# A two-block model in one kernel: the second attention's third turned group placed behind the scores' first 512 columns, and the convolution's high parts made in the first two units

## The reference, cut to what matters

```python
def diff_attend(q, k, v, lam):
    s = jnp.einsum('bqhmd,bkhmd->bhmqk', q, k, preferred_element_type=jnp.float32)
    a = jax.nn.softmax(s * (1.0 / math.sqrt(ATTN_HEAD_DIM)), axis=-1)
    a = a[:, :, 0] - lam * a[:, :, 1]
    return jnp.einsum('bhqk,bkhe->bqhe', a.astype(v.dtype), v)

def head_out(o, subln_g, lam_init):
    return (rmsnorm_2(o, subln_g) * (1.0 - lam_init)).reshape(b, t, ATTN_V_W)
...
    attn = head_out(latent_diff_attention(q, k_all, v_all, lam), subln_g, lam_init)
    conv = short_conv(gb, gc, xc, conv_w)
    out = jnp.einsum('btn,nd->btd', jnp.concatenate([attn, conv], axis=-1), w_out)
```

## Time and profile before

| | us |
|---|---|
| median of three runs | 2697.93 (2696.41 to 2701.72) |
| the profiled execution | 2696.95 |
| its span | 2695.7 |
| TensorE busy in the span | 2598.3 (96%) |
| VectorE busy | 1829.8 (68%) |
| ScalarE busy | 1304.7 (48%) |
| GpSimd busy | 515.2 (19%) |

### The profile page before, as it was taken

How to read it: one execution, slowest core, us unless ns; L and a number is a source line. 1 busy time by engine, 2 the same in 40 slices (tenths; PEclk the granted TensorE clock), 3 DMA queues, 4 the chain that set the end, 5 groups by cost and what they waited for, 6 DMA issues and landing times. The chain is left out here.

```text
span 2695.7 us, 35795 instructions
## 1 busy us (share of the span) xinstructions
PE 2598.3 (96%) x13421; PEld 2202.4 (82%) x13421; DVE 1829.8 (68%) x2193; ACT 1304.7 (48%) x2014; POOL 515.2 (19%) x729
## 2 busy tenths in 40 slices
PE   8999999999999999999999999999997799999996
PEld 7799998888898787778888898778876688888885
DVE  4288887632458888875557333489845788888887
ACT  4255653511343333333445121288723477777775
POOL 5722220000022222221101310022233100000102
PEclk9999999999999999999999999999998899999998
DMA  8700001111323445657655422001144699999998
GB/s 299 268 25 25 24 21 40 47 47 50 123 100 107 148 151 176 198 178 287 202 194 173 110 61 67 5 21 36 67 150 192 236 386 395 395 396 394 395 394 271
DMA packets 249515, 461.90 MB, mean 171 GB/s; under 512 B 16588, under 2 KB 138176, under 8 KB 247936
## 3 DMA queue, kind: packets, MB, share of 16 engines
q1 hardware_dynamic: 218944, 352.73, 37.3%
q0 software_dynamic: 30288, 106.84, 12.1%
q10 hardware_dynamic: 112, 0.03, 0.0%
HBM read 384.79 MB, written 65.32 MB: 167 GB/s over the span
## 5 line engine op out<-in xcount | busy, mean ns | idle before, releaser
L508 PE MATMUL ps<-r,r 128*128 128x512 f32 (+4 forms) x10508 | 2302.0, 377 | 9.1 <-DVE r L672 3.8
L508 PEld LDWEIGHTS ps<-r,r 128*128 128x128 f32 (+1 forms) x10508 | 1879.7, 188 | 360.3 <-issue 9.6
L485 ACT ACTIVATE r<-f 128x2048 fp32r<-128x2048 f32 (+2 forms) x339 | 503.8, 1495 | 386.3 <-PE ps L508 383.2
L3739 DVE TENSOR_TENSOR r<-f,r 128x2048 fp32r<-128x2048 f32 x188 | 429.2, 2291 | 63.8 <-ACT r L485 62.4
L493 DVE TENSOR_TENSOR r<-f,r 128x1024 fp32r<-128x1024 f32 (+1 forms) x151 | 168.1, 1128 | 319.0 <-ACT r L485 319.0
L508 PE MATMUL ps<-f,f 128*128 128x128 f32 (+1 forms) x1218 | 153.3, 277 | 3.9 <-ACT f L1288 3.3
L508 PEld LDWEIGHTS ps<-f,f 128*128 128x128 f32 x1218 | 145.0, 193 | 6.8 <-issue 5.6
L876 DVE SCALAR_TENSOR_TENSOR f<-f,misc,f 128x1023 f32<-128x1023 f32 (+29 forms) x120 | 146.4, 1260 | 0.0
L2018 ACT ACTIVATE r<-f 128x512 fp32r<-128x512 f32 x140 | 87.1, 629 | 71.2 <-PE ps L508 57.4
L3757 POOL DMA_INDIRECT ff_scratch<-f,misc x15 | 29.0, 1934 | 474.1 <-ACT f L3868 442.4
L3269 DVE TENSOR_REDUCE misc<-ps 128x1 f32<-128x1280 f32 x64 | 95.1, 1487 | 21.6 <-PE ps L508 21.3
(11 more groups left out here) (349 smaller groups left out, 2282.8 us busy)
## 6 DMA issues: line engine op xcount, KB each, us to landing
f<-in_w_gate_dram SPq DMA_DIRECT2D x64, 1024.0 KB, 8.3
f<-in_w_up_dram SPq DMA_DIRECT2D x64, 1024.0 KB, 10.1
f<-in_w_down_dram SPq DMA_DIRECT2D x64, 1024.0 KB, 8.0
f<-in_w_in_dram SPq DMA_DIRECT2D x56, 512.0 KB, 4.4
f<-in_w_ada_dram SPq DMA_DIRECT2D x96, 256.0 KB, 4.8
f<-in_w_ffn_in_dram SPq DMA_DIRECT2D x80, 256.0 KB, 4.0
hid_scratch<-f POOLq DMA_DIRECT2D x77, 256.0 KB, 2.8
f<-hid_scratch SPq DMA_DIRECT2D x35, 512.0 KB, 5.0
```

The costliest lines, as they stand in the source:

```text
L485: self.act.activation(hi, raw, ACT.Copy).then_inc(self.sem(st.name + "_hi"), 1)
L508: return self.pe.matmul(o, left, right, start=start, stop=stop, skip_group_check=True)
L3739: self.dve.tensor_tensor(es.lo[i % 4], es.raw[i % 8], es.hi[i % 4].bitcast(F32), ALU.subtract).then_inc(self.sem("e_lo"), 1)
```

## The change

Two edits. On TensorE, in slots 2 to 31, the three transposed groups no longer stand together: groups 0 and 1 come first, then the first 512 columns of the scores of map 1 (two matmuls), then group 2, then the other score columns. On ScalarE the four high parts of the convolution, so far one at the end of each of slots 0 to 3, are made two at the end of slot 0 and two in slot 1 ahead of the second exponential. The semaphores and their counts stay. The orders of VectorE, GpSimd and SyncE are the same as before.

```diff
@@ -3101,31 +3101,32 @@
     def score_sums(self, mp):
         return self.ps[:, 3 * mp:3 * mp + 3, :].rearrange("p a b -> p (a b)")[:, 0:1280]
 
-    def pe_scores2(self, u, mp):
+    def pe_scores2(self, u, mp, parts=(0, 1, 2)):
         pe, sem = self.pe, self.sem
         h, i = self.PAIRS[u]
         sk = self.stacks[h % 2]
-        if u:
+        if u and parts[0] == 0:
             pe.wait_ge(*sem(f"a2_exp{mp}", u))
-        if i == 0:
+        if i == 0 and parts[0] == 0:
             pe.wait_ge(*sem("sk_hi", 6 * (h + 1)))
             pe.wait_ge(*sem("sk_lo", 6 * (h + 1)))
             pe.wait_ge(*sem(f"dma_k{h}", 96))
         q = sk["Q"][mp][:, i * P:(i + 1) * P]
-        for c in range(3):
+        for c in parts:
             cs = slice(c * 512, min(c * 512 + 512, 1280))
             o = self.ps[:, 3 * mp + c, 0:cs.stop - cs.start]
             self.mm(o, q, sk["K"][mp][:, cs], True, False)
             t = self.mm(o, q, sk["L"][mp][:, cs] if c < 2 else sk["C"][mp], False, True)
-        t.then_inc(sem(f"a2_qk{mp}"), 1)
+        if parts[-1] == 2:
+            t.then_inc(sem(f"a2_qk{mp}"), 1)
 
     def pe_attention2(self):
         pe, sem, ps = self.pe, self.sem, self.ps
         n = len(self.PAIRS)
 
-        def turn_p(u):
+        def turn_p(u, groups):
             pe.wait_ge(*sem("a2_mix", u + 1))
-            for g in range(3):
+            for g in groups:
                 k = self.turn_use("p", u, g)
                 self.pe_turn_bank(k)
                 w = (4, 4, 2)[g]
@@ -3160,9 +3161,14 @@
             if u == 2:
 
                 pe.wait_ge(*sem("c2_o", 8))
-            if 2 <= u <= n + 1:
-                turn_p(u - 2)
-            if 0 < u < n:
+            if 2 <= u < n:
+                turn_p(u - 2, (0, 1))
+                self.pe_scores2(u, 1, (0,))
+                turn_p(u - 2, (2,))
+                self.pe_scores2(u, 1, (1, 2))
+            elif n <= u <= n + 1:
+                turn_p(u - 2, (0, 1, 2))
+            if u == 1:
                 self.pe_scores2(u, 1)
             elif u >= n:
                 self.pe_wout2_part(u - n, 1)
@@ -3222,6 +3228,11 @@
                 act.wait_ge(*sem("a2_om", u - 1))
             act.activation(self.SQ2, self.OM2[j], ACT.Square, accum_out=self.sub_ss[j]).then_inc(sem("a2_sq"), 1)
 
+        def high_conv(first, last):
+            for m in range(first, last):
+                ct = (m + 3) % 4
+                act.activation(self.MX[0][:, 4 + ct, :], self.CV[ct], ACT.Copy).then_inc(sem("mc_hi"), 1)
+
         def high_o(u):
             h, i = self.PAIRS[u]
             k = self.turn_use("o", u)
@@ -3248,16 +3259,16 @@
                 elif parts and u > 2:
                     act.wait_ge(*sem("mc_lo", u - 1))
                 self.act_stack(h, parts)
+            if u == 1:
+                high_conv(2, 4)
             if u < n:
                 expo(u, 1)
             if 2 <= u <= n + 1:
                 copy_v(u - 2)
-            if u < 4:
-                if u == 0:
-                    act.wait_ge(*sem("c2_o", 8))
-                    act.wait_ge(*sem("cv2_mm", 24))
-                ct = (u + 3) % 4
-                act.activation(self.MX[0][:, 4 + ct, :], self.CV[ct], ACT.Copy).then_inc(sem("mc_hi"), 1)
+            if u == 0:
+                act.wait_ge(*sem("c2_o", 8))
+                act.wait_ge(*sem("cv2_mm", 24))
+                high_conv(0, 2)
             if u in (3 * NT + 3, 3 * NT + 5):
                 self.act_high_out((u - 3 * NT - 1) // 2)
 
```

## The result

| | median of runs, us | against the kernel before |
|---|---|---|
| before | 2699.96 (19 runs) | |
| changed | 2704.32 (19 runs) | 1.0016, 95% [1.0009, 1.0023] |

The account below looks back on a forecast made before the run. A two-unit loop of 12.69 us bounds the second attention, VectorE the stack slots; -2.15 - 0.25 + 1.47 - 0.4 + 1.1 + 1.2 = +1.0 gives 2697.9, 2698.9 with the runs' median; range 2690.5 to 2704.5.

Parts of the forecast that it names:

- rival 3: Second attention: the lock repeats in both free runs, +4.2, with slots 14 and 22 +7.2, 2702 to 2705; chance 0.2.
- What bounds the kernel: Second attention: a loop over two units of 12.69 us, 6.35 a unit; with stacks VectorE is busy 31.13 of 32.07.
- GpSimd late next: Without the copy wait, TensorE's turned output waits for GpSimd's last operation; loop 12.59, gaining 0.05 a unit, not 0.25.
- the lock repeats: VectorE's mix and GpSimd's last operation exclude each other on shared ports; pitches alternate 5.97 and 7.88, 6.93 a unit.
- 6.14: Pitch in us between first maxima of successive units below which the mix starts before GpSimd's last operation.
- The free runs: Slots 16 to 19: +1.1 (caught +2.5, not -0.3); slots 24 to 31: +1.2 (caught +3.0, not -0.7).
- TensorE's own pitch: Unit pitch after a stall with TensorE on its own: 5.97 us without the copy wait of 0.25, 6.22 with it.
- E + 3.7: TensorE's arrival at the turned output, counted from E, the second exponential's start on ScalarE; 1.04 behind the third group.
- The opening: Convolution's copies moved: -2.15, from 1.75 at M(3) (0.94 copy, 0.8 columns done early) and 0.4 of 0.87.
- Slots 9, 10, with stacks: Slot 9 at 5.97 for 6.22, -0.25; slot 10 caught, +1.47; VectorE-bound slots with stacks, -0.2 twice, -0.4.
- What would show it wrong: L3333 at 0.61 at pitches of 6.0, unit pitches without stacks of 6.0, or unit 1's exponential starting late.
- number 2: Second attention: GpSimd bounds the loop but the lock doesn't repeat, -4.8, 2693.1; chance 0.25.

Follow-up runs that it names:

- scale: Changed kernel with GpSimd's last operation of a unit (output scaled by its norm) made on ScalarE, behind the copies of the turned groups: 2696.86 us, ratio 0.9989.
- scale2: Changed kernel with that output scaling made on ScalarE between the second and third copy of a slot: 2692.05 us, ratio 0.9975 against the kernel before.
- maxfirst: Changed kernel with two VectorE operations swapped, the second maximum of a slot ahead of the mix: 2695.04 us, ratio 0.9987 against the kernel before.
- again2: Changed kernel with two superfluous score matmuls ahead of the first of map 1 in slots 2 to 31: 2705.40 us, ratio 1.002 against the kernel before.
- again1: Changed kernel with one superfluous score matmul ahead of the first of map 1 in slots 2 to 31: 2705.70 us, ratio 1.0024 against the kernel before.
- noeps: Changed kernel without GpSimd's first operation of a unit (the norm's epsilon), its factor put into ScalarE's square: 2700.63 us, ratio 1.0000 against the kernel before.
- part2: Kernel before with only the convolution's edit (high parts two in slot 0, two in slot 1): 2699.13 us, ratio 0.9999.
- part1: Kernel before with only the third group's edit (behind the scores' first 512 columns): 2706.14 us, ratio 1.0031.

## Why the prediction was right, and where it wasn't

The range held the time, by 0.2 us of its upper end (2704.5), which is luck in part, and the change lies within the 0.2% to which I gave 0.65. But what happened in the stage is the main part of rival 3, to which I gave 0.2: both free runs caught, +4.2 in its sum, +4.0 measured. The forecast change was +1.0 and the measured one is +4.4 (the point is 5.4 low, of which 2.0 are the kernel before's own median: 2699.96 over 19 runs, 2697.93 over three). By its steps:

- **What bounds the kernel; GpSimd late next; the lock repeats.** Right. The alternation was put at 7.88 and 5.97 a unit and is 7.88 and 5.82. The steps of the stall came out as worked out: mix to turned output 2.18 (1850.76 - 1848.58), that to the next S 2.35 (1853.11 - 1850.76). Three edits end the repeated hits in three ways, L3344's work on ScalarE (`scale`, `scale2`), the mix moved behind the second maximum (`maxfirst`) and a TensorE above 6.14 (`again2`), and two that leave the pair together keep them (`again1`, `noeps`), so the cause is shown, not only argued.
- **The free runs, "+1.1" and "+1.2".** This is the step that failed. I treated each run start as a coin to be tossed, and took the mean; both were caught, which had its own price in the working, +2.5 and +3.0, measured +2.37 and +2.53. The rows held the answer. At the earlier trace rows L3333 starts 0.02 ahead of the mix. It starts at M(15) + 8.16 (1847.60 - 1839.44), not + 8.05: slot 15 begins while VectorE is still at work, so its mix starts 2.03 behind M(15) instead of 1.91, and the second maximum and the exponential come as much later (5.02 for 4.90). So the limit of the pitch is 8.16 - 1.91 = 6.25 there, not the 6.14 of slot 17. The pitch before was 6.27, and with S 0.1 earlier, as I wrote myself, 6.17: below by 0.08. Measured are a pitch of 6.18 and a margin of 0.07. Slot 24 is the same once more (mix 1901.87, L3344 1901.94). Two such starts that follow one rule are one case, not two halves. VectorE and ScalarE in slot 15 of the kernel before:

```profile
1839.44 1.49 DVE L3269 TENSOR_REDUCE misc<-ps 128x1 f32<-128x1280 f32 x1
...
1841.47 1.55 DVE L3290 SCALAR_TENSOR_TENSOR f<-f,misc,f 128x1280 f32<-128x1280 f32 x1
...
1844.46 1.33 ACT L3194 ACTIVATE f<-ps,misc 128x1280 f32<-128x1280 f32 x1 [1.46 <-DVE misc L3269]
```

- **TensorE's own pitch, "5.97".** Mis-sized: 5.82. I took the 0.25 of idle time from 6.22. In the rows S to turned output is 4.02 before (1854.83 - 1850.81) and 3.56 now (1856.67 - 1853.11), 0.46 less. The other 0.2 is work that overlaps now, as the idle time of a row counts from the modelled end of the matmuls ahead, and without a wait the next one starts before that end: the first score matmul of map 1 starts at 1855.15, 0.24 before the modelled end of the eight transposes.
- **Two sums that came out without following.** I put the two matmuls of the first 512 columns at a third of the six, 0.41; they have 1024 of the 2560 columns, which would be 0.50. The two more of `again2` cost 0.40 a slot. And with 0.25 less and 0.41 more the turned output comes at E + 3.84, not at E + 3.7; in the rows of the changed kernel the third group starts at E + 2.73 (1841.71 - 1838.98, slot 15) and the output 0.95 behind it (1856.67 - 1855.72, slot 17), 3.68 in all.
- **The opening, "-2.15".** The steps to M(3) gave more: 14.42 before, 11.80 now, 2.6 less instead of 1.75, whose two terms (0.94 and 0.8) I had chosen more than worked out. I had let TensorE's work run at half clock; its granted clock was 1.00 here (0.66 before). Why stays open. TensorE idles 1.06 at the place where it idled 1.78, but that doesn't decide it: in the same 10 us (from M(1) + 3.0) the clock is 1.00 in `part2` behind an idle time of 1.54, and 0.83 in `part1` behind 1.06. The rows:

```profile
1750.62 1.33 ACT L3200 ACTIVATE f<-ps,misc 128x1280 f32<-128x1280 f32 x1
...
1751.93 1.54 ACT L3213 COPY f<-ps 128x512 f32<-128x512 f32 x3
1752.09 0.73 PE L508 MATMUL ps<-r,r 128*128 128x512 f32 x2 [1.06 <-ACT f L3200]
...
1757.53 1.48 DVE L3280 TENSOR_REDUCE misc<-ps 128x1 f32<-128x1280 f32 x1
...
1759.43 1.55 DVE L3301 SCALAR_TENSOR_TENSOR f<-f,misc,f 128x1280 f32<-128x1280 f32 x1
1759.67 1.80 POOL L3344 TENSOR_SCALAR f<-f,misc 128x128 f32<-128x128 f32 x1
...
1761.61 0.30 PE L3154 MATMUL ps<-round,f 128*128 128x128 f32 x1 [1.25 <-POOL f L3344]
```

  Then a hit that I had not looked for, in slot 3: M(3) came 5.90 behind M(2), under 6.14. The next pitch is 7.88, and at M(9) 1.54 is left. The rule was in the text and I applied it from slot 9 on only.
- **Slots 28 and 30, where a weight's part delays the copies.** The wait there fell from 1.20 to 0.82, by the 0.4 expected. But the stall stands in the same slots (7.87 and 7.88, for 7.33 and 7.39 before), so each costs only half a microsecond more there: the run of seven is dear in slots 24 and 26 alone.

```profile
1929.56 1.73 POOL L3344 TENSOR_SCALAR f<-f,misc 128x128 f32<-128x128 f32 x1
1930.09 0.41 PE L3134 MATMUL ps<-round,f 128*128 128x128 f32 x2 [0.82 <-ACT f L3213]
```

- **Slots 9, 10, with stacks.** -0.40, +1.40, -0.39 for -0.25, +1.47, -0.4: right. Rival 3's further slots, 14 and 22, were not caught: their pitch is 6.53.
- **What would show it wrong.** Neither exponential came late: they start at 1747.25 and 1750.62, and the maxima that they need ended at 1747.22 and 1750.58.

My reading of the rivals: number 2 (the lock doesn't repeat, 0.25) had the argument that starts in a profile aren't the moment of taking the lock. The rows of `part2` at 0.02 show that this is so, but within a few hundredths only.

The Trainium skill's rule (SBUF — State Buffer, section SBUF: two separate sides), an exclusive lock for a whole instruction, agrees with the runs where VectorE is clearly first: the delayed operation outlasts the mix by 0.47 to 0.49 whether it takes 1.96 or 1.73, and by 0.39 to 0.41 where the two start within 0.04. Where GpSimd is first, VectorE waits for less than the rule says: at a lead of 0.02 the mix takes 0.14 more (1.69), not the 0.6 of GpSimd's whole operation.

## What to carry to other kernels

Before taking a small wait away from the leading engine, ask which two other engines it keeps out of step: find operations that exclude each other, write down the pitch below which they meet, for each stretch from its own rows, and apply it to every slot from the first on. If the kernel runs within 0.1 of that pitch, first move the excluded operation to an engine that runs beside it (here to ScalarE, 0.40 for 0.61), and only then speed up the leader; in one profiled execution each, the same change cost 4.0 us in one surrounding and gave 4.8 in the other. An experiment that shifts one of two racing operations must check that the other doesn't hang on it.

## What the runs showed of the hardware

- Which of the mix and GpSimd's last operation goes first turns at 0.02 us of GpSimd's lead in the rows: from 0.03 on GpSimd's operation took 0.61 in every run, at 0.01 and below, down to the mix being first by 0.69, it took 1.34 to 1.96, and at 0.02 it went either way (0.61 twice before and once in `part2`, 1.96 once in `part2` and once in `again2`).
- Where GpSimd won by less than some 0.15 the mix paid: 1.69 at a lead of 0.02, 1.65 or 1.66 at 0.05, 1.61 at 0.10, 1.57 at 0.14, 1.55 from 0.17 on. The second maximum behind it came up to 0.14 later by that (3.52 behind M(16) in the kernel before, 3.38 behind M(17)), and with it the exponential and GpSimd's next operation.
- The maximum of scores in PSUM doesn't exclude GpSimd: L3344 took 0.61 at 1855.22, within a maximum from 1854.56 to 1856.05.
- GpSimd's smaller operations can be caught too, and by other VectorE operations with two operands in SBUF: one of one column took 1.91 for 0.57 beside the mix in slot 8 of `part1` and 1.67 for 0.55 in slot 8 of `scale2`; in the last slot of the kernel before 2.71 for 0.61 beside two low parts in a row (2.36), whose end it outlasted by 0.40. ScalarE's scaling beside the mix took 0.40.
